# Block 0's start reordered, unread transposes on TensorE, and the remainders of the retention mix split between two engines, in a two-layer GLA and retention trunk

## The reference

```python
h = _rmsnorm(x, norm_w)
z = jnp.einsum('btd,dc->btc', h, w_in).astype(F32)
gq, gk, gv, gg, glr, rq, rk, rv, rg = _split_cols(z)
...
la = (jax.nn.log_sigmoid(glr @ gla_w2.astype(F32) + gla_b.astype(F32)) / GLA_GATE_TAU).reshape(...)
q_b = _rope(rq.reshape(B, T, RET_HEADS, RET_DK), pos)
k_b = _rope(rk.reshape(B, T, RET_HEADS, RET_DK), pos) * (RET_DK ** -0.5)
...
o_a, s_gla_new = _gla_chunked(q_a, k_a, v_a, la, s_gla)     # prompt; _gla_recurrent for the samples
o_b, s_ret_new = _ret_chunked(q_b, k_b, v_b, s_ret)
...
mixed = jnp.concatenate([o_a, o_b], axis=-1).astype(x.dtype)
y = x + jnp.einsum('btc,cd->btd', mixed, w_out)
```

## Time and profile before

| | |
|---|---|
| median of 3 runs | 1674.09 us (1673.62 to 1674.43) |
| the profiled execution | 1673.73 us, of which the span is 1671.9 |
| PE, PEld busy | 1646.9 us (99%), 1349.1 (81%) |
| DVE busy | 1046.5 us (63%) |
| ACT busy | 615.2 us (37%) |
| POOL busy | 854.1 us (51%) |
| chain that ended last | PE 95%, POOL 2%, DVE 1%, DMA 1% |

### The profile page before, as it was taken

The page is one execution under the profiler, slowest core; times in us unless marked ns, Lnnn a source line. Parts: engine busy times, 40 slices in busy tenths (PEclk is TensorE's granted clock), DMA queues, the critical chain, the costliest instruction groups (busy, mean ns, idle before and its releaser), DMA issues.

```text
span 1671.9 us, 26271 instructions
## 1 busy us (share of the span) xinstructions
PE 1646.9 (99%) x9770; PEld 1349.1 (81%) x9770; DVE 1046.5 (63%) x2372; ACT 615.2 (37%) x1159; POOL 854.1 (51%) x661
## 2 busy tenths in 40 slices
PE   6999999999999999999999999999999999999998
PEld 4888778888788887888878888788887888878886
DVE  7743576867765565547755466767887457784474
ACT  4413344233342343423443234342334324342342
POOL 4443645546454464454544445556554545554465
PEclk9999999999999999999999999999999999999999
DMA  7534657656564464366643656466864377453553
GB/s 265 166 105 100 177 201 224 181 162 176 181 186 129 103 198 138 114 155 160 190 133 96 155 140 187 164 176 182 194 184 139 114 163 161 161 170 105 142 156 138
DMA packets 384096, 266.33 MB, mean 159 GB/s; under 512 B 286560, under 2 KB 288992, under 8 KB 383968
## 3 DMA queue, kind: packets, MB, share of 16 engines
q1 hardware_dynamic: 310096, 130.14, 30.9%
q10 hardware_dynamic: 73872, 134.51, 24.6%
HBM read 217.51 MB, written 47.05 MB: 158 GB/s over the span
## 4 chain that ended last, share of the span: by engine, by line
PE 95%; POOL 2%; DVE 1%; DMA 1%; ACT 0%; issue 0%; ACTq 0%; POOLq 0%; SPq 0%
PE bank L718 82%; PE bank L977 3%; PE bank L983 2%; PE bank L781 1%; PE bank L961 1%; PE bank L939 1%; POOL w_lo L272 1%; PE bank L918 1%; PE bank L685 1%; POOL m_lo L652 1%; PE bank L922 1%; PE bank L739 1%; PE bank L994 0%; PE bank L791 0%; PE bank L897 0%; DMA w_stage<-in_w_slots 0%
## 5 line engine op out<-in xcount | busy, mean ns | idle before, releaser
L272 POOL TENSOR_TENSOR w_lo<-w_stage,w_hi 128x512 fp32r<-128x512 f32 x264 | 369.3, 1419 | 327.0 <-ACT w_hi L265 326.9
L718 PE MATMUL bank<-h_hi,w_hi 128*128 128x512 f32 x1024 | 408.5, 399 | 4.2 <-DVE h_lo L355 4.2
L718 PE MATMUL bank<-h_lo,w_hi 128*128 128x512 f32 x1024 | 399.8, 390 | 0.0
L718 PE MATMUL bank<-h_hi,w_lo 128*128 128x512 f32 x1024 | 399.4, 390 | 0.0
L272 POOL TENSOR_TENSOR w_lo<-ss,w_hi 128x512 fp32r<-128x512 f32 x164 | 223.0, 1380 | 206.4 <-ACT w_hi L265 206.2
L265 ACT ACTIVATE w_hi<-w_stage 128x512 fp32r<-128x512 f32 x264 | 152.9, 624 | 372.5 <-PE bank L718 326.2
L718 PEld LDWEIGHTS bank<-h_hi,w_hi 128*128 128x128 f32 x1024 | 192.5, 188 | 55.6 <-issue 8.1
L718 PEld LDWEIGHTS bank<-h_hi,w_lo 128*128 128x128 f32 x1024 | 192.6, 188 | 41.1
L718 PEld LDWEIGHTS bank<-h_lo,w_hi 128*128 128x128 f32 x1024 | 192.8, 188 | 37.2
L718 PE MATMUL bank<-w_hi,m_hi 128*128 128x512 f32 x512 | 201.7, 394 | 2.5 <-POOL m_lo L652 1.9
L718 PE MATMUL bank<-w_hi,h_hi 128*128 128x512 f32 x512 | 201.1, 393 | 0.0
(11 more groups left out here) (217 smaller groups left out, 2215.6 us busy)
## 6 DMA issues: line engine op xcount, KB each, us to landing
w_stage<-in_w_slots ACTq DMA_DIRECT2D x264, 256.0 KB, 3.5
ss<-in_w_slots ACTq DMA_DIRECT2D x164, 256.0 KB, 3.6
v_b<-in_w_slots ACTq DMA_DIRECT2D x84, 256.0 KB, 3.4
region<-in_x_prompt SPq DMA_DIRECT2D x32, 512.0 KB, 4.4
out_o_rows<-region SPq DMA_DIRECT2D x64, 256.0 KB, 3.5
region<-out_o_rows SPq DMA_DIRECT2D x192, 64.0 KB, 3.1
xn<-in_x_t SPq DMA_DIRECT2D x16, 512.0 KB, 4.9
out_k_rows<-region SPq DMA_DIRECT2D x32, 256.0 KB, 3.9
```

Source lines behind the costliest of these rows:

```text
L272: pool.tensor_tensor(w_lo[:, r, c], stage(h), w_hi[:, r, c].bitcast(f32), ALU.subtract).then_inc(lo_done, 1)
L718: i = pe.matmul(P[q][:, :], x, y, start=(s == 0 and kk == 0 and c == 0), stop=(s == 3 and kk == 1 and c == 2), skip_group_check=True)
```

## The change

It touches five places.

1. `idle_turns`: 36 transposes of the identity into a bank that nobody reads, 10, 18 and 8 of them on PE between the factor transposes, behind them, and behind the first K tile's three products of slot 1.
2. ACT's and POOL's order ahead of the loop: h_hi of tile 0 right behind the first weight half, weight halves 2 and 3 rounded one tile earlier, POOL's w_lo 2 and 3 ahead of the sample's factor.
3. In block 0 `hT_slot0` goes behind slot 2, with the sample's gate products behind it; the gate's expansion, the sample's small matmuls and all that follows from them (ACT's logarithms, DVE's decays) move one slot later.
4. In block 0 `next_stats` goes from w = 2 to w = 8 on DVE. The retention queries (`queries`) are split off from `rotate` and go ahead of the second half's decays.
5. In all blocks m_lo of retention tiles 2 and 3 goes from POOL to DVE (w = 24), and POOL's second one from w = 23 to w = 24.

```diff
+        def idle_turns(pe, count):
+            for _ in range(count):
+                pe.transpose(X[:, 0:128], ident[:, :], ident[:, :])
...
             for t in range(TPB):                              # scale_rows
                 if m == 0 and t % 2 == 0:
+                    if t > 0:
+                        idle_turns(pe, 10)
                     pe.wait_ge(first_rs, t // 2 + 1)
...
             i.then_inc(ht_ps.sem, KT)
+            if m == 0:
+                idle_turns(pe, 18)
...
                             products(0, 0, 0, (k,))           # first_slot
+                            if k == 0:
+                                idle_turns(pe, 8)
...
-                            if n == 0 and u == 0 and s == 1:  # unit_slot
-                                if q == 0:
-                                    sample_transposed(0)
-                                if q == 1:
-                                    gate_expand()
-                                if q == 2:
-                                    sample_gate()
+                            if n == 0 and w == 2 and q == 0:
+                                sample_transposed(0)
+                            if n == 0 and w == 3 and q == 0:
+                                gate_expand()
...
                             first_slot()
-                            hT_slot0()
                             continue
...
+                        if n == 0 and w == 2:
+                            hT_slot0()
...
             split_hi(act, 0)
+            next_hi(act, 0, 0)
             split_hi(act, 1)
-            load_half(act, 4)
-            load_half(act, 5)
-            for k in range(KT):
+            for k in range(1, KT):
                 next_hi(act, 0, k)
-                if k in (3, 5):
-                    split_hi(act, (k + 1) // 2)
+                if k == 1:
+                    load_half(act, 4)
+                    load_half(act, 5)
+                if k in (2, 3):
+                    split_hi(act, k)
...
-                        if w == 2:
+                        if w == 2 + late:                     # ACT's logarithms; late = int(n == 0)
...
-                        if w in (3, 4):
-                            hf = w - 3
+                        if w == 5:
+                            queries()
+                        if w in (3 + late, 4 + late):
+                            hf = w - 3 - late
...
-                        if w == (2 if n == 0 else 1) and n < NBLK - 1:
+                        if w == (8 if n == 0 else 1) and n < NBLK - 1:
                             next_stats(vec, n + 1)
...
-                        for h in {23: (0, 1), 24: (2,), 25: (3,)}.get(w, ()):
+                        if w in (23, 24):                     # POOL
+                            h = w - 23
                             pool.wait_ge(mhi_sb.sem, mhi_sb.at(n, h + 1))
-                            pool.tensor_tensor(m_lo[:, 4 + h, :], ret_t[h], ..., ALU.subtract).then_inc(mlo_sb.sem, 1)
+                            pool.tensor_tensor(m_lo[:, 4 + h, :], ret_t[h], ..., ALU.subtract).then_inc(mlo_first.sem, 1)
...
+                        if w == 24:                           # DVE
+                            mixed_rest_ret(2)
+                            mixed_rest_ret(3)
```

More of the change, by code:

```diff
@@ L618, in _ @@
                 split_lo(pool, h)
+            for h in range(2, 2 * AHEAD):
+                split_lo(pool, h)
             pool.wait_ge(s_v.sem, s_v.at(0, V_NV - V_LAST))
             rsqrt(srs[:, :], svar[:, :], s_p.sem)
-            for h in range(2, 2 * AHEAD):
-                split_lo(pool, h)
             for l in range(DEPTH):
@@ L643, in body @@
                             rsqrt(xrs_1[:, n - 1, :], yvar[:, :], rstd_y.sem)
-                        if w == 8 and n < NBLK - 1:
+                        if w == (9 if n == 0 else 8) and n < NBLK - 1:
                             pool.wait_ge(xstat.sem, xstat.at(n + 1, 4))
@@ L686, in hT_slot0 @@
                         i.then_inc(slot_used, 1)
-                        if kind == 0 and n > 0:
+                        if kind == 0:
                             sample_gate()
@@ L1090, in sample_work @@
                             nc.scalar.activation(gt[:, :], gt[:, :], ACT.Ln, bias=1.0).then_inc(gl_s.sem, 1)
[L1091 to L1092 removed]
+                        if w in (7 + late, 14, 22, 26):
+                            c = (7 + late, 14, 22, 26).index(w)
                             col = (0, 8, 4, 12)[c]
@@ L1104, in sample_work @@
                                                      ACT.Tanh, scale=0.5).then_inc(tg_s.sem, 1)
+                    late = int(n == 0)
                     for w in range(SLOTS):
-                        if w == (1 if n > 0 else 2):
-                            act.wait_ge(slot_used, n * SLOTS + (1 if n > 0 else 2) + RING)
+                        if w == (1 if n > 0 else 3):
+                            act.wait_ge(slot_used, n * SLOTS + w + RING)
                             act.wait_ge(const_in, 96)
@@ L1141, in body @@
                         sample_work(w)
-                        if w == 2:
+                        if w == 2 + late:
                             for hf, src in ((0, ATT), (1, OB)):
@@ L1260, in _ @@
                     sample_mean(0)
-                if k == 7:
+                if k == 6:
                     sample_norm(0)
-            vec.wait_ge(const_in, 96)
-            vec.tensor_scalar(gmask[:, :], rmask[:, 0:TOK], 0.0, None, ALU.is_gt)
             for l in range(DEPTH):
@@ L1405, in sample_work @@
                         if kind == 0:
-                            if w == 4:
+                            if w == 4 + late:
                                 sample_gate()
@@ L1593, in mixed_rest, with mixed_rest_ret, queries @@
                     def mixed_rest(h):
-                        vec.wait_ge(mlo_sb.sem, mlo_sb.at(n, 4))
                         vec.wait_ge(mhi_sb.sem, mhi_sb.at(n, 4 + h + 1))
                         vec.tensor_tensor(m_lo[:, h, :], o_t[:, h, :], m_hi[:, h, :].bitcast(f32), ALU.subtract).then_inc(mlo_sb.sem, 1)
-                    def rotate():
+                    def mixed_rest_ret(h):
+                        vec.wait_ge(mhi_sb.sem, mhi_sb.at(n, h + 1))
+                        vec.tensor_tensor(m_lo[:, 4 + h, :], ret_t[h], m_hi[:, 4 + h, :].bitcast(f32), ALU.subtract).then_inc(mlo_sb.sem, 1)
+                    def queries():
                         for p in range(2):
@@ L1628, in rotate @@
                             c += 4
+                    late = int(n == 0)
                     if n == 0:
                         sample_start(l)
+                        vec.wait_ge(const_in, 96)
+                        vec.tensor_scalar(gmask[:, :], rmask[:, 0:TOK], 0.0, None, ALU.is_gt)
                     for w in range(1, SLOTS):
```

26 lines of the change are left out of this document (17 added, 9 removed).

## The result

The changed kernel takes 1679.43 us (median of 7 runs, 1678.37 to 1681.01), the kernel before 1674.09 (7 runs, 1673.58 to 1674.89). The ratio is 1.0031, 95% interval 1.0022 to 1.0041: slower, by 5.3 us at the medians. The profiled execution took 1679.66 us, its span is 1677.9, 6.0 more than before. The forecast was 1682.0, its range 1675.5 to 1685.5.

The account below looks back on a forecast made before the run. PE was taken to bound the kernel, busy for 1646.9 of 1671.9 us. 1673.73 + 6.0 (stall) + 1.4 (clock) + 0.9 (remainders) = 1682.0 us, range 1675.5 to 1685.5.

Parts of the forecast that it names:

- The stall in slot 9: Block 0: statistics on DVE between turned keys and first score mask delay PE's outputs by 6.0 us (bounds +2 and +7.5).
- the 5 to 7.5 that were to show the forecast right: Sign for the forecast: PE waits 5 to 7.5 us at block 0's first outputs, released by DVE's mask.
- The clock: Behind PE's idle time in slot 9 of block 0, products run at half level: +1.4 us (bounds 0 and 1.7).
- The remainders: m_lo split between POOL and DVE: 1.9 us of waits removed, 2.8 lost in blocks 1 and 5, together +0.9.
- The start: Kernel's start: PE enters slot 3 about 1.4 us earlier (bounds 0 and 2.5), a gain not on the path that counts.
- The wait for the sample's normalised input: Block 0, slot 2: PE waits 0.9 us for the input that DVE makes behind h_lo tile 6.
- without the clock's fall: Slot 9's stall without the lower clock, 1680.6 us, or with keys earlier and a short insert about 1677; chance 0.22.
- rival 2: Faster: keys land long before PE's slot 8, so the statistics are hidden; 1670.4 or 1671.8 us; chance 0.10.
- The transposes with no effect on the clock: At the start, transposes don't raise the level; costs 1.6 us, swallowed by slot 9, still 1682; chance within the forecast's 0.55.
- rival 1: Slot 9's stall without the clock's fall or with a short insert: 1680.6 or about 1677 us; chance 0.22.
- rival 4: Worse: in blocks 1 and 5 each DVE operation waits for POOL, and the insert is 7.2 us: 1685.7; chance 0.13.

## Why the prediction held, point by point

The direction, the place and the mechanism were right: one stall of PE in slot 9, made by the statistics between keys and mask, and the clock's fall behind it. The total of 1682.0 is 2.6 us above the median of 1679.43. Three terms of the sum were off. The stall's 1.2 us too much and the clock's 1.4 too little cancel, so the 2.6 us of the total are those of the remainders. With the measured terms the sum is 1673.73 + 4.8 + 2.8 - 1.7 = 1679.6 us.

- **The stall in slot 9, forecast +6.0, measured +4.8.** The keys came 0.76 us earlier (0.5 taken). That this is so near is luck. The rotation began at 48.78 and not at 48, four of its eight operations up to the second tile of keys took 1.5 to 1.7 us, beside POOL's w_lo, where before only one did, and the tile was ready at 58.51 instead of 54.92. The way out to DRAM and back made up for it. DVE and SP in the changed kernel, against the earlier trace rows:

```profile
57.82 0.69 DVE L1652 TENSOR_TENSOR region<-region,tmp 128x512 f32<-128x512 f32 x1
```

```profile
53.84 5.04 SPq L450 DMA_DIRECT2D out_k_rows<-region  x2
60.76 7.91 SPq L455 DMA_DIRECT2D k_n<-out_k_rows  x16
```

  From the second tile to the way back it is 2.25 us (58.51 to 60.76) and was 5.71, and from there to the keys 10.34 and was 11.23. The insert was 5.8 us (6.5 taken, and 5.8 was named as the value if POOL doesn't hold the last operation). It didn't: the last operation took 0.16 us here (79.12) against 1.22 in the earlier trace rows, beside no operation of POOL. The stretching moved to the queries' copies, of which two lines take 1.39 and 1.20 us above, beside POOL's w_lo. The mask came 5.0 us later, and the margin of 0.3 us came off, which the working had left in. PE idled for 4.56 us and not for about 7, below the 5 to 7.5 that were to show the forecast right, because the stall was shorter and the start's gain was gone by then.
- **The clock, forecast +1.4, measured +2.8 (2.7 by the transposes in the stall).** The level does fall, and that was taken from the eight slow products of the start. The mis-sized part is how long it stays down. I carried over the number of products, eight; here PE ran at half level for 5.9 us, from 83.58 to about 89.5, whereas at the start it was 16.40 to some 20 us. The Trainium skill, "TensorE: Matmul & The Clock Gate", Part 1, says that activity releases the throttle and that an idle engine falls back; the granted clock of 0.50 behind the idle time, and of 1.00 once it was filled, agrees. For the price it was the measured stretch that counted.
- **The remainders, forecast +0.9, measured about -1.7.** The sign was wrong. By the starts of the slots of all blocks, summed, the waits that went gave 3.6 us and not 1.9, and the two new waits cost 1.2 in block 1 and 0.7 in block 5, 1.9 and not 2.8. (DVE's two subtractions in block 1 took 3.29 us beside POOL, but the two sample groups behind them 2.09 where they had taken 4.69.) The first error is in how I read the waits list. One of the seven places in the kernel before:

```profile
604.26 0.39 PE L718 MATMUL bank<-w_hi,m_lo 128*128 128x512 f32 x1
604.84 0.47 PE L718 MATMUL bank<-w_hi,m_hi 128*128 128x512 f32 x1 [0.19 <-POOL m_lo L652]
605.15 0.40 PE L718 MATMUL bank<-w_lo,m_hi 128*128 128x512 f32 x1
```

  Products follow each other at 0.23 us; here 0.58 and 0.31 lie between them, so 0.43 us is lost where 0.19 is listed. Of the other 0.24, 0.16 is how the list counts: the idle time begins at the recorded end of the product before, 0.39 us behind its start, though the next would have started after 0.23. The last 0.08 is the longer distance behind the wait. Five of the seven places lose 0.43 us each, the two with 0.5 us listed 0.85, 3.85 together for a listed 1.9; 3.6 of it came through. It holds for the long waits too (in block 1 of the changed kernel PE's product before the gate tile starts at 401.51, the one behind it at 403.69, 2.18 us apart for a listed 1.79), where it hardly matters.
- **The start, forecast 1.4 us earlier at slot 3 and swallowed in slot 9.** It was 1.1 at slot 1 and 0.7 at slot 4. It was gone at slot 8 already, because al stood behind the rotation on DVE, and PE's turn behind slot 7 waited for it. For the time that made no difference here. That it never could, since slot 9 sets itself by DVE, was too strong: in the trace without the transposes a start 0.7 us later came back as keys 1.5 us later. The wait for the sample's normalised input was forecast at 0.9 us and measured at 1.02. The products of the start spaced at 0.23 are as forecast, that PE then waits 1.06 us for the sample's mean was missed.

Against the rivals: without the clock's fall (1680.6 or 1677) is nearer to the measured time than the forecast by the number, but wrong by its mechanism: the clock did fall, and the time is low because of the remainders. The statistics are not hidden in slot 8, as rival 2 had it, but they are in slot 7, one slot away. The transposes with no effect on the clock is false, with no effect on the time is true within what these runs can tell. Two ends of the range were added up wrongly: rival 1's own terms (keys 1.5 us earlier than taken, insert 1.0 shorter) give 1678.1 and not about 1677, and rival 4 adds 1.5 for an insert that its own 7.2 makes 0.7 longer.

The balance: 4.76 + 2.82 between outputs and slot 10, and -1.6 from there to the end, is 6.0, the difference of the spans. The medians differ by 5.3 only: the profiled execution of the kernel before lies 0.4 under its median, that of the changed kernel 0.2 above. Of the experiments' differences against each other some tenths are of the same kind.

## What to carry to other kernels

Work that is moved to where an engine is idle must be put ahead of the instruction that it idles on: one slot earlier, the same 5.8 us cost nothing. Before an insert is judged harmless, look for the next thing that the other engine needs from this one, and its margin (0.3 us here). A stall of some us of the matmul engine costs its length and then the clock, 4.8 and 2.8 here, while a short wait costs more than the list says, here 0.24 us in most cases.

## What the runs showed of the hardware

- After 4.56 us of idling TensorE ran at half level for 5.9 us, although it was busy all that time; gaps of about 1 us (18.94, and 0.98 in front of the outputs in the kernel with transposes there) did not lower it, nor did one of 1.86 us ahead of 25.32 in that same kernel, behind which products are spaced at 0.23.
- 36 unread transposes took 4.09 us at full level, 0.11 each, and kept it there: the granted clock behind them reads 1.00; with idling in their place it reads 0.50.
- The column of the granted clock does not show every fall. Where the clock fell within the run it reads 0.50. At the kernel's start it reads 1.00 in the kernel before, although products are spaced at 0.43 us; there the spacing is the thing to read.
